# Layer norms of a fused two-block kernel: sums of squares by token, with one-column products, and a weight rounding moved behind them

## The reference, cut to what matters

```python
def layer_norm(x, g, b):
    xf = x.astype(jnp.float32)
    mu = jnp.mean(xf, axis=-1, keepdims=True)
    xc = xf - mu
    var = jnp.mean(xc * xc, axis=-1, keepdims=True)
    return (xc * lax.rsqrt(var + LN_EPS) * g.astype(jnp.float32) + b.astype(jnp.float32)).astype(x.dtype)

# for each layer i
x = layer_norm(ALPHA * x + mix.astype(x.dtype), ln_mix_g[i], ln_mix_b[i])
x = layer_norm(ALPHA * x + swiglu(x, w_ffn_gate[i], w_ffn_up[i], w_ffn_down[i]), ln_ffn_g[i], ln_ffn_b[i])
gate = jax.nn.sigmoid(x @ w_ple_gate[i] + b_ple_gate[i])
x = x + (p[i] @ w_ple[i]) * gate
```

## Time and profile before

| | us |
|---|---|
| median of 3 runs (lowest to highest) | 2537.39 (2536.77 to 2538.65) |
| the profiled execution, its own time | 2534.19 |
| its span in the trace | 2532.5 |

### The profile page before, as it was taken

One profiled execution on the slowest core, in us unless ns is written; L12 is line 12 of the kernel. 1 busy time (PEld: TensorE's weight loads), 2 busy tenths in 40 slices (PEclk: granted clock), 3 DMA queues, 4 the chain that ended last, 5 costly groups with the idle time before them and its releaser, 6 DMA issues.

```text
span 2532.5 us, 32937 instructions
## 1 busy us (share of the span) xinstructions
PE 2445.0 (97%) x13536; PEld 1985.1 (78%) x13536; DVE 1702.5 (67%) x1814; ACT 1208.1 (48%) x1445; POOL 410.6 (16%) x285
## 2 busy tenths in 40 slices
PE   8998996999999999899999999999999999999998
PEld 5677883888888888687767769989878776989976
DVE  4785545888888888545476559749454647956835
ACT  3433233778787877322345345325252555524424
POOL 1001011101010100000000016336100012715410
PEclk9999998999999999999999999999999999999999
DMA  7223214899999999412211212232232002223320
GB/s 281 73 92 124 100 62 159 313 371 366 365 353 361 357 365 341 169 68 100 83 50 50 68 57 100 94 115 97 96 116 100 34 17 76 100 92 117 109 112 38
DMA packets 64727, 388.98 MB, mean 154 GB/s; under 512 B 13376, under 2 KB 13504, under 8 KB 22720
## 3 DMA queue, kind: packets, MB, share of 16 engines
q1 hardware_dynamic: 53856, 373.20, 40.0%
q0 software_dynamic: 9280, 8.42, 1.0%
q10 hardware_dynamic: 1440, 5.24, 0.5%
HBM read 391.00 MB, written 20.97 MB: 163 GB/s over the span
## 4 chain that ended last, share of the span: by engine, by line
PE 91%; DVE 4%; ACT 2%; DMA 2%; issue 1%; POOL 0%; DVEq 0%; SPq 0%; POOLq 0%; ACTq 0%
PE psD L3279 57%; PE psD L2376 8%; PE psA L2376 8%; PE psA L3279 2%; PE psA L2360 1%; PE psA L1164 1%; PE psD L3287 1%; PE psA L3354 1%; PE psA L3512 1%; PE psA L3287 1%; DVE ring_r L2885 1%; PE psA L3572 1%; DMA ring<-w_dense 1%; ACT ring_r L2671 1%; PE psA L2455 1%
## 5 line engine op out<-in xcount | busy, mean ns | idle before, releaser
L3279 PE MATMUL psD<-rounded,ring_r 128*128 128x512 f32 (+1 forms) x3192 | 759.4, 398 | 5.1 <-DVE ring_r L2885 3.2
L3279 PEld LDWEIGHTS psD<-rounded,ring_r 128*128 128x128 f32 (+1 forms) x3192 | 594.2, 187 | 165.2 <-issue 14.9
L3279 PE MATMUL psD<-ring_r,rounded 128*128 128x512 f32 (+1 forms) x1728 | 408.0, 392 | 4.6 <-DVE rounded L1050 2.4
L3279 PEld LDWEIGHTS psD<-ring_r,rounded 128*128 128x128 f32 x1728 | 316.9, 189 | 84.4 <-issue 7.2
L1045 DVE TENSOR_TENSOR ring_r<-ring,ring_r 128x2048 fp32r<-128x2048 f32 x128 | 293.1, 2290 | 43.0 <-ACT ring_r L843 40.9
L843 ACT ACTIVATE ring_r<-ring 128x2048 fp32r<-128x2048 f32 x128 | 245.3, 1917 | 50.7 <-PE psD L3279 25.9
L2671 ACT ACTIVATE ring_r<-ring 128x2048 fp32r<-128x2048 f32 (+2 forms) x71 | 131.8, 1856 | 208.7 <-PE psD L3279 182.6
L2885 DVE TENSOR_TENSOR ring_r<-ring,ring_r 128x2048 fp32r<-128x2048 f32 (+2 forms) x71 | 159.0, 2239 | 88.4 <-ACT ring_r L2671 86.5
L2376 PE MATMUL psD<-rounded,fast_r 128*128 128x256 f32 x1680 | 199.9, 279 | 0.0
L2376 PE MATMUL psA<-rounded,fast_r 128*128 128x256 f32 x1680 | 199.6, 279 | 0.0
L2376 PEld LDWEIGHTS psA<-rounded,fast_r 128*128 128x128 f32 x1680 | 198.1, 188 | 0.4
(11 more groups left out here) (475 smaller groups left out, 2930.3 us busy)
## 6 DMA issues: line engine op xcount, KB each, us to landing
ring<-w_moe SPq DMA_DIRECT2D x192, 1024.0 KB, 7.1
ring<-w_dense SPq DMA_DIRECT2D x134, 1024.0 KB, 4.8
ring<-w_dense SPq DMA_DIRECT2D x16, 768.0 KB, 3.9
ring<-w_dense SPq DMA_DIRECT2D x16, 640.0 KB, 3.7
arena<-x_t SPq DMA_DIRECT2D x1, 2048.0 KB, 8.0
token_rows<-arena ACTq DMA_DIRECT2D x4, 512.0 KB, 2.6
arena<-pair_rows SPq DMA_DIRECT2D x4, 512.0 KB, 7.9
arena<-pair_rows ACTq DMA_DIRECT2D x4, 512.0 KB, 8.6
```

Source lines behind the costliest of these rows:

```text
L3279: mm = pe.matmul(out, w[a], x[b], start=start and i == 0, stop=stop_ and i == 2)
```

## The change

The sums of squares swap their operands. A chunk of squares, 128 channels by 128 tokens, is now the stationary operand and one column of ones the moving one: for each tile k and chunk m a product of one column, which adds 128 tokens' sums to column m of the bank. That is 32 products in place of 8. They are preceded by one product of four columns of zeros (`strict_u`'s first column is zero), which clears the four columns, since the four sums interleave in one bank. The result already has tokens on the partitions, so that `by_token` goes and the scaling reads the bank. One stand-in of 512 columns is put ahead of the wait for `stat`, in the norms of the second part. In the two "mix" norms the rounding of the unit of `("gu", layer, 1)` moves from behind the means into the loop of step 5, ahead of the scaling of tile 4.

```diff
@@ VectorE, layer_norm @@
                 dve.nop().then_inc(freed(m_), 1)
-                ahead.leave(("down", layer, 1, 3) if which == "ffn" else (("mix_out", 3), ("wo", 3))[layer])
+                if which == "ffn":
+                    ahead.leave(("down", layer, 1, 3))
                 ready(dve, v_)
-                by_token(v_, ln_part(n))
-                step(dve.tensor_scalar(stat, stat, 1.0 / D, 1e-5, ALU.mult, ALU.add))
+                take(v_, dve.tensor_scalar(stat, bank(v_)[:, 0:NCH], 1.0 / D, 1e-5, ALU.mult, ALU.add))
                 inv_sqrt(dve.nop(), stat)
                 dve.nop().then_inc(sem("stat"), 1)
                 ready(dve, b_)
                 for k in range(KT + 1):
+                    if k == 4 and which == "mix":
+                        ahead.leave((("mix_out", 3), ("wo", 3))[layer])
                     if k < KT:
@@ TensorE, layer_norm @@
                 out = aux(("lnv", which, layer))
+                pe.matmul(out[:, 0:NCH], ones, strict_u[:, 0:1].to_broadcast([P, NCH]), start=True, stop=False,
+                          skip_group_check=True)
                 for k in range(KT):
                     pe.wait_ge(sem("ln_sq"), KT * n + k + 1)
-                    mm = pe.matmul(out, ones, SQ2K[:, k, :], start=(k == 0), stop=(k == KT - 1))
+                    for m in range(NCH):
+                        mm = pe.matmul(out[:, m:m + 1], SQ2K[:, k, P * m:P * m + P], ones[:, 0:1], start=False,
+                                       stop=(k == KT - 1 and m == NCH - 1), skip_group_check=True)
                 filled(mm)
-                spread_stat(("lnb", which, layer), n + 2)
+                spread_stat(("lnb", which, layer), n + 2, 1)
@@ TensorE, spread @@
-            def spread(name, count):
+            def spread(name, count, stand_ins=0):
 
                 out = aux(name)
+                keep_clock(out, stand_ins)
                 pe.wait_ge(sem("stat"), count)
```

## The result

The change makes the kernel slower: 2562.47 us, median of 4 runs (2555.42 to 2565.40), against 2538.02 (2536.77 to 2540.16) for the kernel before beside it. The ratio is 1.0086, 95% interval 1.0069 to 1.0104, so 24.5 us. The forecast was 2556.8, with a range of 2541 to 2564. The profiled execution took 2563.45 us.

What follows compares the result with a forecast made beforehand. TensorE was taken to bound the kernel (91% of the span). Norm 0 +4.5, norm 2 +5.7 and the ffn norms 9.2 give +19.4 us: 2553.6 on the profiled 2534.2, 2556.8 as median; range 2541 to 2564.

Steps and rivals of the forecast that it cites:

- sums of squares, with the clock's fall: One-column products in all four norms, partly at half clock: +5.4 us in each mix norm, +4.0 in each ffn norm.
- gap ahead of the spreading: Wait between sums of squares and spreading shrinks to 1.4 us: -1.8 us in each mix norm, -1.0 in each ffn norm.
- the spreading: Products that spread the statistics, at half clock: +0 and +0.5 us in the mix norms, +0.9 in each ffn norm.
- products behind, and the moved rounding: After the spreading: clock back in mix norms, -1.1 and -0.3 us; rounding stall +1.95 each; ffn norms +0.7 each.
- The 60 cycles: Skill's figure for products up to 64 columns; by it the sums would end some 2 us sooner in each norm.
- two short stretches elsewhere in the kernel: Narrow products on TensorE: 64 columns, clock falling to 0.50 from 231.9; 39 columns, 3.6 us, all at 0.50.
- the 6.3 us at half clock behind norm 0: Kernel before: clock read as returning 6.3 us after wide products resumed; so expected back after the changed kernel's spreading.
- Behind the rounding wait a load on SyncE's queue and GpSimd's sums: Mix norms: these start some 11 us later, near 1505, need about 5 us, first reader at 1518.37: cost nothing.
- The clock holds: Rival: full clock through the one-column products; 4.9 us faster, 2532.5 us; chance 0.12.
- It falls in two norms only: Rival: clock falls only in ffn norms, +6.3 us, 2543.7, or only in mix norms, +8.2, 2545.6; chance 0.05.
- One-column records keep their speed at half clock: Rival: clock falls but records in the sums stay at 0.11 us; in all +1.8 us, 2539.2; chance 0.03.
- The rounding doesn't stall TensorE: Rival: no stall in mix norms, up to 3.9 us off the forecast, 2552.9; inside the forecast's range, no own chance.

Runs made afterwards that it cites:

- the first experiment: The change with the rounding of the mix norms left in its old place: 2552.2 us, ratio 1.0046 against the kernel before.
- The move alone: The kernel before with only the rounding moved into the loop, wide float32 sums of squares kept: 2544.63 us, ratio 1.0023.

## Why the prediction was right

It held in sign, size and main cause: the half clock of the one-column records. By its steps, summed over the four norms (measured: the two profiled executions; the fourth row is what is left of 21.1):

| step | forecast, us | measured, us |
|---|---|---|
| sums of squares, with the clock's fall | +18.8 | +15.2 |
| gap ahead of the spreading | -5.6 | -4.3 |
| the spreading | +2.3 | +1.8 |
| products behind, and the moved rounding | +3.9 | +8.4 |
| all | +19.4 | +21.1 |

That the sum came so close is partly luck: the first row was forecast 3.6 us too dear and the fourth 4.5 us too cheap, and the two errors all but cancel.

*Records.* 0.112 us at full clock was forecast and found. At half clock 0.213 was taken from 39-column products, and 0.208 found. By the formula of the Trainium skill (TensorE: Matmul & The Clock Gate, "LDWEIGHTS (loading the stationary operand)"), which has the number of columns in it and no term for the clock, a load of 128 columns is estimated at 107 ns. At full clock the trace agrees (0.112 us a record); at half clock (0.208) it doesn't. The 60 cycles that I had quoted for up to 64 columns are in the Trainium skill (same page, "Back-to-back issue gap") the figure for an isolated product; for a stream of weight loads and products the same section says that both set the spacing, and the 0.112 us do not speak against that.

*The clock.* It fell in all four norms, as forecast from two short stretches elsewhere in the kernel. They were thin ground for it: the one at 423.82 began at half clock behind 8.74 us of idle time, so it shows the price and not a fall, and the one at 228.5 had 0.69 us idle in it. That the clock can fall in one-column products without an idle gap was first shown by norms 1 and 3 of the change. The place was off: 5.2 us behind the last wide product in norm 0 and 2.1 in norm 2, where I had used 3.2, and 4.0 and 4.9 in norms 1 and 3, where I had used 3.7. So norm 2 paid more than forecast (13.28 us for 12.5) and the other three less (10.5, 10.3 and 9.5 for 12.5, 11.0 and 11.0). From one execution to the next it shifts again: the changed kernel's second profile has the fall in norm 0 1.3 us sooner. No finer forecast was to be had from rows of one execution. One reading was wrong, without effect on the sum: the 6.3 us at half clock behind norm 0 of the kernel before are counted from the spreading (1498.88 on), whose products have 128 columns. The wide products resume at 1500.72, so the clock was back some 4.3 us behind them.

*Gap and scaling.* The gap is 1.7 us, for a forecast 1.4: the stand-in's two records start with the end of the last narrow one and hold the spreading back by 1.85 us (1506.96 to 1508.81). The scaling takes 0.16 us in all four norms (VectorE, line 1988), as forecast, but not for the reason given: the first experiment has it at 0.16 with the rounding in its old place. The clearing product hides in the mix norms and delays the others by 0.14 us (1868.24 to 1868.38 in norm 1), for a forecast 0.22.

*The moved rounding: mis-sized.* The step "Behind the rounding wait a load on SyncE's queue and GpSimd's sums", priced at "nothing", failed. I had asked when the sums' reader needs them, and not what runs on VectorE while they run. The stall was 3.29 and 3.30 us where 1.95 was forecast and 2.3 was the upper bound. The low part of tile 3 grew by 1.65 us (2.40 for 0.75), which with 1.95 makes 3.6; a little is VectorE's lead. Each stall of the change was also followed by a second fall of the clock, 3.4 us at 0.50, in both of its profiles; the kernel with the rounding in its old place has no second fall in any norm. (Without the stand-in, norm 0 had the stall and no second fall, so a stall does not always bring one.) Stalls and falls are most of the fourth row's 8.4. The move alone confirms it: +6.9 us in its trace. The hint stood in the earlier trace rows, where the scaling takes 1.01 us beside GpSimd's sum and 0.17 without; I read it as a wait that would go, and GpSimd's sums moved to a worse place.

*The rivals.* The clock holds: out, in every profile of this form by token in float32 but for the two ffn norms of the kernel with 512-column stand-ins. It fell in norms 1 and 3 of the change with no idle gap just ahead, so idle gaps, by which this rival would have won, do not decide it alone. It falls in two norms only: out. One-column records keep their speed at half clock: out, by 0.112 against 0.208 us a record, and by 13.2 against 23.0 us for the same stream with stand-ins. The rounding doesn't stall TensorE: out.

What stays open: why the clock falls sooner in one norm than in another and shifts between executions; whether it would hold in norms 0 and 2 if the 1.3 us of idle time ahead of the sums were filled, which no run tried; and the 5 us between the two comparisons of the change.

## What to carry to other kernels

Count the records and weight loads of a product, not its columns: a one-column float32 record cost 0.11 us at full clock and 0.21 at half. So a tile's four one-column products, eight records with 1/128 of the columns, cost as much as its one wide product at full clock (0.90 us for 0.87), and nearly twice that at half (1.66). A busy TensorE is no assurance of its clock; where wide work gives way to narrow, or to a gap, look at the granted clock there, and price both levels. And when an operation on VectorE is moved, follow what it releases on other engines: GpSimd's work, started at the wrong time, stretched operations of VectorE up to threefold.

## What the runs showed of the hardware that I had not expected

- The clock fell with TensorE 99 to 100% busy and no idle gap: in norm 3, 4.9 us into one-column products that followed directly on wide ones.
- Filler didn't bring a lost clock back while the narrow products went on: 23.9 us at 0.50 with 512-column stand-ins between the tiles. The same stream, entered from wide products without a gap, kept its clock for all of its 13.2 us.
- A low part on VectorE, with both inputs in on-chip memory (SBUF), waited for the end of a GpSimd sum under way, 2.40 us for 0.75. Operations with an input in PSUM did not: a tile's scaling took 0.73 us and the scaling of the statistics 0.16 us beside such sums.
- With every instruction ahead of norm 0 the same, it began anywhere from 1482.4 to 1493.0 us in 14 profiles.
